# A hybrid scan / attention / expert-retrieval step on one core: value products with the value tile stationary and the transposed result turned back at the end

## What is computed

```python
def block(x):
    q = (x @ w_q).reshape(n, P_HEADS, 2, P_QDIM // 2)
    s = jnp.einsum('nhjd,hjkd->nhjk', q, sub_keys).astype(jnp.float32)
    sv, si = lax.top_k(s, P_TOPK)
    ...
    gate = jax.nn.softmax(tv, axis=-1).astype(x.dtype)
    u = u_tab[eidx]
    act = jax.nn.gelu(jnp.einsum('nhkd,nd->nhk', u, x), approximate=False)
    return jnp.einsum('nhk,nhkd->nd', gate * act, v_tab[eidx])
```

## Time and profile before

| | |
|---|---|
| median of 3 executions | 2973.16 us (2967.1 to 2978.52) |
| span of the profiled execution, first to last instruction | 2953.0 us (its whole device time isn't listed; the median is 20.2 us above the span) |
| PE busy | 2846.8 us, 96% |
| PEld busy | 2508.5 us, 85% |
| DVE busy | 1953.2 us, 66% |
| ACT / POOL busy | 1027.6 us, 35% / 960.8 us, 33% |
| v stage of layer 0 | 1096.6 to 1576.1 us of the span |
| v stage of layer 1 | 2459.6 to 2940.2 us of the span |

### The profile page before, as it was taken

How to read it: one execution, slowest core, us unless ns; L and a number is a source line. 1 busy time by engine, 2 the same in 40 slices (tenths; PEclk the granted TensorE clock), 3 DMA queues, 4 the chain that set the end, 5 groups by cost and what they waited for, 6 DMA issues and landing times.

```text
span 2953.0 us, 47696 instructions
## 1 busy us (share of the span) xinstructions
PE 2846.8 (96%) x18222; PEld 2508.5 (85%) x18222; DVE 1953.2 (66%) x4284; ACT 1027.6 (35%) x1428; POOL 960.8 (33%) x695
## 2 busy tenths in 40 slices
PE   7989999999999999999998979999999999999998
PEld 4966658999999998888887868999999998888886
DVE  3876654687862237888886475487774225888887
ACT  4611104333453332222224264333354333222222
POOL 0000000137887703233220000117887721242420
PEclk9999999999999999999999989999999999999999
DMA  6346634866787778998983304677678778898984
GB/s 247 108 147 228 221 109 143 294 187 172 178 232 172 175 237 269 312 321 298 323 276 120 115 16 137 206 252 177 148 209 201 176 188 273 295 321 301 313 299 160
DMA packets 340183, 631.63 MB, mean 214 GB/s; under 512 B 73808, under 2 KB 221392, under 8 KB 337696
## 3 DMA queue, kind: packets, MB, share of 16 engines
q1 hardware_dynamic: 140960, 428.57, 45.0%
q0 software_dynamic: 81024, 99.92, 13.7%
q10 hardware_dynamic: 118016, 100.67, 10.7%
HBM read 533.37 MB, written 95.35 MB: 213 GB/s over the span
## 4 chain that ended last, share of the span: by engine, by line
PE 91%; DVE 5%; DMA 2%; ACT 1%; issue 1%; another core or an unknown queue 1%; SPq 0%; DVEq 0%; ACTq 0%
PE ps L1218 32%; PE ps L613 15%; PE ps L615 15%; PE ps L614 15%; DMA ring<-in_ada 2%; PE ps L1192 1%; PE ps L586 1%; DVE arena L1657 1%; PE ps L723 1%; PE ps L674 1%; PE ps L1165 1%; PE ps L705 1%; PE ps L790 1%; DVE hslab L1657 1%
## 5 line engine op out<-in xcount | busy, mean ns | idle before, releaser
L1657 DVE TENSOR_TENSOR w_lo<-ring,w_hi 128x1024 fp32r<-128x1024 f32 x576 | 701.6, 1220 | 508.8 <-ACT w_hi L1306 496.7
L613 PE MATMUL ps<-hT_hi,w_hi 128*128 128x384 f32 x2576 | 867.8, 337 | 5.4 <-ACT arena L1582 5.3
L614 PE MATMUL ps<-hT_lo,w_hi 128*128 128x384 f32 x2576 | 861.3, 334 | 0.3 <-issue 0.3
L1218 PE MATMUL ps<-w_hi,ga_parts 128*128 128x512 f32 x2560 | 846.8, 395 | 1.0 <-DVE ga_parts L1657 1.0
L615 PE MATMUL ps<-hT_hi,w_lo 128*128 128x384 f32 x2384 | 797.2, 334 | 0.0
L1306 ACT ACTIVATE w_hi<-ring 128x1024 fp32r<-128x1024 f32 x378 | 400.0, 1060 | 946.7 <-PE ps L615 751.9
L1218 PE MATMUL ps<-w_lo,ga_parts 128*128 128x512 f32 x1536 | 606.0, 395 | 0.0
L1218 PEld LDWEIGHTS ps<-w_hi,ga_parts 128*128 128x128 f32 x2560 | 482.3, 188 | 114.6 <-issue 2.4
L613 PEld LDWEIGHTS ps<-hT_hi,w_hi 128*128 128x128 f32 x2576 | 484.0, 188 | 9.0 <-issue 8.4
L614 PEld LDWEIGHTS ps<-hT_lo,w_hi 128*128 128x128 f32 x2576 | 484.2, 188 | 1.1 <-issue 0.6
L615 PEld LDWEIGHTS ps<-hT_hi,w_lo 128*128 128x128 f32 x2384 | 448.0, 188 | 0.0
(11 more groups left out here) (339 smaller groups left out, 2353.4 us busy)
## 6 DMA issues: line engine op xcount, KB each, us to landing
ring<-in_u SPq DMA_DIRECT2D x256, 512.0 KB
ring<-in_v SPq DMA_DIRECT2D x256, 512.0 KB
ring<-in_ada SPq DMA_DIRECT2D x96, 512.0 KB
act_dram<-arena SPq DMA_DIRECT2D x256, 192.0 KB
arena<-g_dram ACTq DMA_DIRECT2D x32, 1280.0 KB
arena<-act_dram ACTq DMA_DIRECT2D x32, 1280.0 KB
g_dram<-arena POOLq DMA_DIRECT2D x24, 1024.0 KB, 24.3
ring<-in_mix_in SPq DMA_DIRECT2D x42, 512.0 KB
```

Of the source, the lines that this page charges most:

```text
L613: pe.matmul(out, hi[:, c, :], hT_hi[:, c, :], start=(c == 0), stop=False)
L614: pe.matmul(out, hi[:, c, :], hT_lo[:, c, :], start=False, stop=False)
L1218: mm = pe.matmul(ps[:, 2 * t + nb, :], l_, r_[:, cs], start=(first and q == 0), stop=(last and q == len(pairs) - 1), skip_group_check=True)
L1657: return dve.tensor_tensor(out, a, b, op)
```

## The change

The operands of the v stage change places. The chunk `w_hi` or `w_lo` (128 experts x 128 channels) is stationary, and the 320 tokens' gate-activations, high or low part, are streamed: 8 chunks x 3 = 24 matmuls of 320 columns per tile, into 8 PSUM banks, channels on partitions. DVE's split has one subtraction of 320 columns in place of two. After the last tile each bank is scaled by the gate (a per-partition number now) on its way out of PSUM into `out_T`, even chunks by ACT, odd ones by DVE, and PE turns it back by 24 matmuls of 128 columns against the identity. The near sums are multiplied with their gate on DVE and folded in by two matmuls; the residual on DVE is one addition. The residuals go half by half (`ROWS_PEER`), not token tile by token tile. Ahead of the last two tiles PE waits once for the gate-activations of tile 127. In layer 0 the split of the next projection's first two tiles moves ahead of the scaling on both engines.

```diff
-ROWS_PEER = [(nb, t) for t in range(3) for nb in range(2)]
+ROWS_PEER = [(nb, t) for nb in range(2) for t in range(3)]
...
-        ps_copy = area(22528, D)
+        out_T = hslab[:, 0:DC * T].rearrange("p (c t) -> p c t", c=DC)
...
-                def v_products(t, nb, n, hi, lo, first=False, last=False):
+                def v_products(n, c, hi, lo, first=False, last=False):
+
+                    high_, low_ = (ga_parts[:, n % 2, at:at + DENSE] for at in (0, DENSE))
+                    cs = slice(c * P, (c + 1) * P)
+                    for q, (l_, r_) in enumerate(((hi, high_), (hi, low_), (lo, high_))):
+                        mm = pe.matmul(ps[:, c, 0:DENSE], l_[:, cs], r_, start=(first and q == 0), stop=(last and q == 2))
                     return mm
...
                     pe.wait_ge(ga_ready, (NJ * layer + n + 1) + it * step)
+                    for c in range(DC):
+                        if first and c == 6:
+                            pe.wait_ge(gelu_done, NJ * (layer + 1))
+                        mm = v_products(n, c, hi, lo, first)
+                    mm.then_inc(multiplied, 1)
+
+                def rows_of(nb):
+
                     for t in range(NT):
...
+                        bank = 3 * nb + t
+                        pe.wait_ge(v_taken_act if bank % 2 == 0 else v_taken_dve, DC // 2 * layer + bank // 2 + 1)
+                        if t == 0:
+                            pe.matmul(ps[:, bank, :], folds[:, 64:192], v_sum[:, 512 * nb:512 * nb + 512], start=True, stop=False,
+                                      skip_group_check=True)
...
+                        for q in range(4):
+                            mm = pe.matmul(ps[:, bank, q * P:(q + 1) * P], out_T[:, 4 * nb + q, t * P:(t + 1) * P], ident,
+                                           start=(t > 0 and q == 0), stop=True, skip_group_check=True)
+                        mm.then_inc(v_rows_ready, 1)
...
+                ends = [split_landed(g0 + n, 0) for n in (NJ - 2, NJ - 1)]
+                pe.wait_ge(ga_ready, NJ * layer + NJ)
+                for c in range(DC):
+                    for n, (hi, lo) in zip((NJ - 2, NJ - 1), ends):
+                        mm = v_products(n, c, hi, lo, last=(n == NJ - 1))
+                    if c == DC - 1:
+                        mm.then_inc(multiplied, 2)
+                    else:
+                        mm.then_inc(v_T_ready, 1)
+                    if c == 6:
+                        pe.wait_ge(folds_ready, layer + 1)
+                        pe.wait_ge(near_scaled, layer + 1)
+                        rows_of(0)
+                rows_of(1)
...
-                act.wait_ge(tile0_done, layer + 1)
-                for nb in range(2):
-                    act.activation(ps_copy[:, 512 * nb:512 * nb + 512], ps[:, nb, :], ACT.Copy).then_inc(tile0_copied, 1)
+                if layer == 0:
+                    for n in range(2):
+                        high(stage_tiles(1)["mix_in"] + n)
+                for c in range(0, DC, 2):
+                    act.wait_ge(v_T_ready, (DC - 1) * layer + c + 1)
+                    act.activation(out_T[:, c, 64:P], ps[:, c, 0:64], ACT.Copy, scale=mods[:, layer, 40 + c, 0:1])
+                    act.activation(out_T[:, c, P:T], ps[:, c, 64:DENSE], ACT.Copy, scale=mods[:, layer, 40 + c, 1:2]).then_inc(v_taken_act, 1)
...
                 for k, (nb, t) in enumerate(ROWS_PEER):
...
+                    dve.wait_ge(v_rows_ready, 6 * layer + k + 1)
                     if k == 4:
                         normalise(2 * layer + 2, 0)
-                    residual(2 * layer + 1, k, nb, t, 2 * t + nb if t else 6 + nb)
+                    cols = slice(512 * nb, 512 * nb + 512)
+                    tt(x[:, t, cols], x[:, t, cols], ps[:, 3 * nb + t, :], ALU.add).then_inc(x_updated, 1)
...
-                    tt(ga_parts[:, k % 2, T:2 * DENSE], ga[:, k % 2, 64:DENSE], ga_parts[:, k % 2, P:T].bitcast(F32), ALU.subtract)
-                    tt(ga_parts[:, k % 2, 0:64], ga[:, k % 2, 0:64], ga_parts[:, k % 2, 64:P].bitcast(F32), ALU.subtract).then_inc(ga_ready, 1)
+                    tt(ga_parts[:, k % 2, DENSE:2 * DENSE], ga[:, k % 2, :], ga_parts[:, k % 2, 0:DENSE].bitcast(F32), ALU.subtract)\
+                        .then_inc(ga_ready, 1)
...
+                dve.wait_ge(rows_summed, PER_ROW * (layer + 1))
+                tt(v_sum, v_sum, gatef[:, 0:D], ALU.mult).then_inc(near_scaled, 1)
+                dve.memset(out_T[:, :, 0:64], 0.0)
+                if layer == 0:
+                    for n in range(2):
+                        low(stage_tiles(1)["mix_in"] + n)
+                for c in range(1, DC, 2):
...
+                    dve.tensor_scalar(out_T[:, c, 64:P], ps[:, c, 0:64], mods[:, layer, 40 + c, 0:1], None, ALU.mult)
+                    dve.tensor_scalar(out_T[:, c, P:T], ps[:, c, 64:DENSE], mods[:, layer, 40 + c, 1:2], None, ALU.mult).then_inc(v_taken_dve, 1)
```

More of the change, by code:

```diff
@@ L1225, in v_tile @@
                     pe.wait_ge(ga_ready, (NJ * layer + n + 1) + it * step)
-                    for t in range(NT):
-                        for nb in range(2):
[L1228 to L1235, removed]
+                    for c in range(DC):
[4 more added lines that the diff above has]
+                def rows_of(nb):
+                    for t in range(NT):
+                        bank = 3 * nb + t
[3 more added lines that the diff above has]
+                                      skip_group_check=True)
+                        if t == 0 and nb == 0:
+                            pe.wait_ge(v_taken_act, DC // 2 * layer + 2)
+                            pe.wait_ge(v_taken_dve, DC // 2 * layer + 2)
+                        if t == 0 and nb == 1:
+                            pe.wait_ge(v_taken_act, DC // 2 * layer + 4)
+                            pe.wait_ge(v_taken_dve, DC // 2 * layer + 4)
+                        for q in range(4):
+                            mm = pe.matmul(ps[:, bank, q * P:(q + 1) * P], out_T[:, 4 * nb + q, t * P:(t + 1) * P], ident,
+                                           start=(t > 0 and q == 0), stop=True, skip_group_check=True)
+                        mm.then_inc(v_rows_ready, 1)
                 g0 = at + NJ
@@ L1639, in _ @@
                 peer(layer)
-                if layer == 0:
-                    for n in range(2):
-                        high(stage_tiles(1)["mix_in"] + n)
                 norm_stats_by_half(2 * layer + 2, ROWS_PEER)
@@ L1759, in after_mix @@
                     elif t < NT - 1:
-                        dve.wait_ge(rows_done, 4 + 2 * nb + t + 1 if layer else nb + 1)
+                        dve.wait_ge(rows_done, 2 + 2 * nb + t + 1 if layer else nb + 1)
                     else:
@@ L2425, in peer @@
                             add_row(GATHER_AT[2 * GJ * r + j])
+                dve.wait_ge(rows_summed, PER_ROW * (layer + 1))
[5 more added lines that the diff above has]
+                for c in range(1, DC, 2):
+                    if c < DC - 1:
+                        dve.wait_ge(v_T_ready, (DC - 1) * layer + c + 1)
+                    else:
+                        dve.wait_ge(multiplied, g0 + NJ)
+                    dve.tensor_scalar(out_T[:, c, 64:P], ps[:, c, 0:64], mods[:, layer, 40 + c, 0:1], None, ALU.mult)
+                    dve.tensor_scalar(out_T[:, c, P:T], ps[:, c, 64:DENSE], mods[:, layer, 40 + c, 1:2], None, ALU.mult).then_inc(v_taken_dve, 1)
             dve.memset(silu8, 0.0)
```

18 lines of the change are left out of this document (6 added, 12 removed).

## The result

The changed kernel takes 2931.49 us (median of 4 executions, 2929.16 to 2934.3); the kernel before, run beside it, 2975.36 (4 executions, 2967.1 to 2978.52). The ratio is 0.9866, 95% interval 0.9845 to 0.9887: 1.3% or 40 us faster, 34 to 46 by the interval, where 47 us were forecast. The two medians by themselves lie 43.9 us apart. The profiled execution took 2933.7 us, with a span of 2931.1.

The account below looks back on a forecast made before the run. PE's unbroken matmuls were taken to bound both v stages. Products -60, transfers +3 and ends +10 sum to -47 us, so 2973 became 2926 us; range 2910 to 2958, the forecast's own 2909 to 2946.

Parts of the forecast that it names:

- Its likeliest case: Whole kernel: the forecast itself, 2926 us, with its own range of 2909 to 2946; given 72%.
- each of its marks: Signs of being right: 3024 matmuls in some 438 us, PEld near 100% busy, DVE standing some 4 us for the first root.
- Part 1, the products: V stage on PE: 24 matmuls of 320 columns replace 16 of 512 per tile; 60 us gained over 252 tiles.
- the straight line: V products: step at 320 columns from a line through the u stage's 384 and the v stage's 512; 0.1438 us.
- the surplus of 384 kept: V products: step at 320 columns if the u stage's surplus at 384 columns stays; 0.1467 us.
- Part 2, the loads: V stage: 24 weight loads per tile in place of 16, costed at nothing, since 0.114 us each is below 0.145.
- Part 3, DVE: V stage: DVE's split and additions need 3.13 us a tile over seven tiles, below PE's 3.48; nothing due.
- Part 4, transfers: V stage: 331 GB/s needed at a share of 0.98, fits closely; 3 us lost, bounds 0 and 20.
- transfers set the pace: Rival, v stage: 312 GB/s is a ceiling, so only 15 tiles per layer gain; 2970 us; 12%.
- Part 5, the ends: End of each layer's v stage: 4.7 us longer per layer, 10 us for both; bounds 3 and 17.
- the sum for the first root: Layer's end: 1.6 + 4 x 1.06 + table load 1.28 + 0.3, put at 7.2 us after the last product.
- The 1 us for a lower clock at the next projection: After the v stage: 1 us for longer idle ahead of the next projection, first matmuls at the lower clock, and layer 1's normalise.

Follow-up runs that it names:

- token-order run: The changed kernel with the residuals put back in the old order, token tile by token tile, products and turning kept as changed; 2904.92 us.

## Why the prediction was right, and where a term was off

By medians it was 2926 for 2931.49, by the difference -47 for -40 (-43.9 between the medians). Its likeliest case is the one that happened, and each of its marks is in the profile: the piece of 3024 matmuls (443.62 us for some 438), PEld at 100% in the steady stretch, DVE standing 3.91 us for the first root (some 4).

- **Part 1, the products: -60 forecast, -50 measured.** 252 x (3.718 - 3.521) = 49.6. This is the term that failed, in its size. The text had three values, 0.1438, 0.1467 and 0.1524, and took 0.145, a compromise between the straight line and the surplus of 384 kept, with the reason "384 is the nearer shape". By that reason the value was 0.1467, and it is what the trace shows to the digit. The line through two rows was no law: the runs at 256 and 512 columns show a level and a step up, not a slope. The surplus is 12 to 20 ns at all four widths. The Trainium skill ("TensorE: Matmul & The Clock Gate", Back-to-back issue gap) has 2.5 ns over the columns, but for an isolated matmul; for a stream of matmuls with a load each it gives some 131 ns at 512 columns, less than the columns alone. No fp32r row here shows either: the step at 512 is 228 to 233 ns.
- **Part 2, the loads: nothing, and it was nothing.** The price rested on the plain fp32 rows of 0.114; the run at 256 columns shows the same for fp32r, 0.1188. The Trainium skill ("Trainium Kernel Development and Optimization", Best Practices) would read the distance to the limit off the loads' busy share and the MFU, the share of the peak arithmetic that is reached. Here the loads' share was 100% at steps of 0.173, 0.147 and 0.119 alike (at 0.119 from 1110 to 1132 us of the run with 256 columns), so in these traces a full PEld says nothing of a bound.
- **Part 3, DVE: nothing due.** Predicted 3.13 us a tile on average; busy 3.03. No product waited for DVE's own work inside the steady stretch.
- **Part 4, transfers: +3 forecast, about 0.** The rate needed was put at 331 GB/s; the stretch from 1200 to 1500 us shows 330. The kernel before had one stop of some 1.0 us (layer 1), the changed one has one of 0.94 (layer 0). The rival "transfers set the pace" had the right neighbour and the wrong distance: the run with 256 columns reached 339 GB/s at 3.40 us a tile, so 312 is no ceiling. The 352 GB/s of the earlier trace rows, which spoke against it, is of a stretch with other transfers, and no v stage here reached it over 300 us.
- **Part 5, the ends: +10 forecast, +9.3 measured.** From tile 125's end to the next projection 28.4 us for 23.7, +4.7 per layer as worked out; layer 1's the same, 28.3 us to the end of the span for 23.6. By its steps: to the last product 11.82 (11.7 forecast, 10.87 before), where the wait for tile 127 is 1.0 us as put; from there to the last root 10.7 (11.2 forecast, 7.4 before); and 0.5 more behind it. The mechanism was only half of it: the text has the order of halves as the reason, and the token-order run shows that order to be 1.5 of the 3.3 us. The rest is that all six statistics now stand behind the last product, where before one stood ahead of it, and that the first of them starts 1.3 us after it. A slip stands in the sum for the first root: its terms add up to 7.4 us, not 7.2; 6.9 was measured. The 1 us for a lower clock at the next projection was not due: before and after show the same ten or so steps of 0.32 us there.
- **The sum.** -50 + 0 + 9.3 = -41, against -40 measured. Of the 10 us too many on the products, 3 for transfers that did not come and 0.7 of the ends took a part back, and this was luck; 6 were left between -47 and -41. The upper end of the forecast's own range, 2946, does not come from its bounds as they stand: steps of 0.1467 with 20 for transfers and 17 for the ends give 2960.

The profiled span of before lay 20.2 us under its median, and the profile didn't say why. A span lies only 2 to 3 us below its own execution's time (2931.1 and 2933.7), so that execution was a shorter one than the median's; comparing the two spans alone would have made the change 22 us.

## What to carry to other kernels

Where a shape lies near one whose step the trace has, take that shape's surplus over its columns, rather than a line through two shapes; shorter and more numerous matmuls are then priced by columns plus that surplus, and the loads behind them are priced from the shortest step that any row shows, not from the length or busy share of their rows. When a product loop gets faster, look for the transfer that is issued one buffer ahead: its time to land against the new time of one buffer's work tells where the next stops will come from. And an order written for one end of a stage (by token tile, by halves) has to be worked out again when what arrives last changes: here halves cost 2.5 us per layer, and moving all that doesn't need the last chunk ahead of it gave 5.

## What the runs showed of the hardware

- A matmul in fp32r with a load of its own costs 12, 13, 13 and 20 ns over its columns at 256, 320, 384 and 512 (15 in one stretch of 512); at 512 it is 19 with the operands the other way round. With two of three products in bf16, whose loads' rows are half as long (97 for 188 ns), a cycle of three is 7 ns shorter, an estimated 3 to 4 ns for each bf16 product.
- Loads whose rows last 188 ns are hidden down to a step of 0.119 us.
- With the ring, the gathers and the loads of gates and activations together, the v stage of the run with 256 columns ran at 339 GB/s and a share of 0.97; one 1280 KB load of the activations then takes 24 to 29 us to land (19 at the one place read in the run without the gathers).
- Behind a stop of 5.0 us PE ran at a granted clock of 0.50, with some 0.21 us a step at 256 columns in place of 0.119; behind a row of shorter ones that ended in one of 4.2 us, 0.32 in place of 0.173 at 384.
